# Two kinds of attention heads whose items alternate on one core

## What is computed

```
def diff_attention(q, k, v, lam):      # 6 heads, two components of width 32
    s = einsum('bqhcd,bkhcd->bhcqk', q, k) * DA ** -0.5
    p = softmax(s);  w = p[:, :, 0] - lam * p[:, :, 1]
    return einsum('bhqk,bkhe->bqhe', w, v)
def softmax_attention(q, k, v):        # 6 heads of width 96
    p = softmax(einsum('bqhd,bkhd->bhqk', q, k) * QK_C ** -0.5)
    return einsum('bhqk,bkhe->bqhe', p, v)
o_a = rmsnorm(diff_attention(...), subln_a) * (1 - l_init)
y = concatenate([o_a, conv, o_c]) @ w_out
```

## Time and profile before

| | us |
|---|---|
| median of 3 runs (lowest, highest) | 2022.19 (2021.28, 2024.68) |
| the profiled execution | 2023.35 |
| its span in the trace | 2021.3 |
| attention loop of layer 0, first score to first OC transpose | 217.7 to 402.3 |
| attention loop of layer 1 | 1119.9 to 1302.2 |

### The profile page before, as it was taken

The page is one execution under the profiler, slowest core; times in us unless marked ns, Lnnn a source line. Parts: engine busy times, 40 slices in busy tenths (PEclk is TensorE's granted clock), DMA queues, the critical chain, the costliest instruction groups (busy, mean ns, idle before and its releaser), DMA issues.

```text
span 2021.3 us, 28791 instructions
## 1 busy us (share of the span) xinstructions
PE 1836.7 (91%) x11300; PEld 1638.5 (81%) x11300; DVE 1407.1 (70%) x2038; ACT 1029.0 (51%) x1401; POOL 328.3 (16%) x507
## 2 busy tenths in 40 slices
PE   5999778799999999998998678897999999999994
PEld 3987666698999999998987566696788888888883
DVE  5375885537665656646466885536888888888987
ACT  4235686625121121124235786534777777777772
POOL 0082541001000000001083530200000000000002
PEclk9999799999999999999999899997999999999997
DMA  9125300023544445421221000006999999999995
GB/s 342 57 93 189 109 1 1 22 84 115 167 157 136 156 136 167 133 82 53 70 78 48 1 1 1 2 22 250 391 399 398 409 408 387 404 388 404 377 392 218
DMA packets 112438, 366.21 MB, mean 181 GB/s; under 512 B 7456, under 2 KB 65216, under 8 KB 85936
## 3 DMA queue, kind: packets, MB, share of 16 engines
q1 hardware_dynamic: 94448, 303.50, 40.1%
q0 software_dynamic: 13536, 48.39, 6.9%
q10 hardware_dynamic: 4320, 12.49, 1.6%
HBM read 349.23 MB, written 15.12 MB: 180 GB/s over the span
## 4 chain that ended last, share of the span: by engine, by line
PE 74%; DVE 13%; ACT 7%; DMA 3%; issue 2%; POOL 0%; SPq 0%; POOLq 0%; DVEq 0%; ACTq 0%
PE PS L2446 27%; PE PS L2335 25%; PE PS L2003 5%; PE PS L2390 5%; PE PS L2427 4%; ACT E L909 3%; PE PS L2126 3%; PE PS L2091 3%; DVE NM L1354 2%; DVE KCn L1301 1%; DVE split L1637 1%; ACT PT L914 1%; DMA raw<-in_w_ada_head 1%; DVE SS L1284 1%; DVE QC L1301 1%
## 5 line engine op out<-in xcount | busy, mean ns | idle before, releaser
L2446 PE MATMUL PS<-H,split 128*128 128x320 f32 x2304 | 339.7, 309 | 1.6 <-DVE H L1901 1.6
L2446 PEld LDWEIGHTS PS<-H,split 128*128 128x128 f32 x2304 | 338.1, 188 | 3.1 <-DVE H L1901 2.3
L1088 ACT CAST split<-raw 128x2048 fp32r<-128x2048 f32 (+2 forms) x64 | 112.8, 1763 | 228.5 <-PE PS L2446 184.4
L1637 DVE TENSOR_TENSOR split<-raw,split 128x2048 fp32r<-128x2048 f32 (+2 forms) x64 | 138.1, 2162 | 123.9 <-ACT split L1088 123.7
L1548 DVE TENSOR_TENSOR msplit<-raw,msplit 128x2048 fp32r<-128x2048 f32 x82 | 187.9, 2292 | 36.4 <-ACT msplit L1045 36.4
L1548 DVE TENSOR_TENSOR split<-raw,split 128x2048 fp32r<-128x2048 f32 x82 | 186.8, 2290 | 18.1 <-ACT split L1045 18.0
L2335 PE MATMUL PS<-split,HT 128*128 128x512 f32 x816 | 195.7, 396 | 3.7 <-DVE HT L1527 2.4
L1045 ACT CAST msplit<-raw 128x2048 fp32r<-128x2048 f32 x82 | 157.0, 1914 | 69.7 <-PE PS L2335 60.0
L2335 PE MATMUL PS<-msplit,HT 128*128 128x512 f32 x816 | 191.2, 390 | 0.6 <-DVE msplit L1548 0.6
L2003 PE MATMUL PS<-split,H 128*128 128x384 f32 (+1 forms) x960 | 171.3, 340 | 12.8 <-DVE split L1637 9.5
L2003 PEld LDWEIGHTS PS<-split,H 128*128 128x128 f32 x960 | 169.4, 195 | 14.5 <-DVE split L1637 10.7
(11 more groups left out here) (352 smaller groups left out, 3035.2 us busy)
## 6 DMA issues: line engine op xcount, KB each, us to landing
raw<-in_moe_w_gate SPq DMA_DIRECT2D x55, 1024.0 KB, 7.5
raw<-in_moe_w_down SPq DMA_DIRECT2D x55, 1024.0 KB, 7.9
raw<-in_moe_w_up SPq DMA_DIRECT2D x54, 1024.0 KB, 7.3
DOTW<-in_w_ada_rows POOLq DMA_DIRECT2D x56, 512.0 KB, 4.0
raw<-in_w_ada_head SPq DMA_DIRECT2D x16, 1024.0 KB, 7.0
mraw<-in_moe_w_up SPq DMA_DIRECT2D x14, 1024.0 KB, 7.3
mraw<-in_moe_w_gate SPq DMA_DIRECT2D x13, 1024.0 KB, 7.4
mraw<-in_moe_w_down SPq DMA_DIRECT2D x13, 1024.0 KB, 7.8
```

The costliest lines, as they stand in the source:

```text
L1088: A.copy(split[u % 2][:, 0, 0:w], src[:, 0:w]).then_inc(S["split_hi"], 1)
L1637: V.tensor_tensor(split[u % 2][:, 1, 0:w], src[:, 0:w], split[u % 2][:, 0, 0:w].bitcast(f32), ALU.subtract).then_inc(S["split_lo"], 1)
L2446: ins = T.matmul(PS[:, 4 * (u % 2) + 2 * c + hf, 0:HALF], W[:, w, k, c * P:(c + 1) * P], A(a, k, hf), start=(k == 0 and w == 0 and a == 0) ...
```

## The change

The items get a new order. Heads 0 and 1 run alone, then four blocks of ten alternate the items of heads 2 and 6, 3 and 7, 4 and 8, 5 and 9, then heads 10 and 11 run alone. Scores, semaphore values, outputs and groups now go by tables made from that order. Values of a block are paired within a kind (items 0 and 2, 1 and 3, 4 and 6, 5 and 7 of the block; 8 and 9 single), so that PT has a third buffer. LT leaves `split` and lies in two of the raw slots, those of the third and fourth w_out chunk, and SP loads these two only when the layer's last score is done. The subln work moves to the steps 50 to 55, two tiles a step; the mixing transposes to 55 to 59; the first chunk's rounding to 53 (ACT) and 54 (DVE).

```diff
-K_SUM, K_ROOT, K_NORM, K_OUT = A_ITEMS + 4, A_ITEMS + 14, A_ITEMS + 16, ITEMS - NT - 1
-K_MIX = ITEMS - NT - 2
+K_SUM, K_NORM = {50: (0,), 51: (1, 2), 52: (3, 4)}, {53: (0,), 54: (1, 2), 55: (3, 4)}
+K_ROOT, K_OUT, K_MIX, K_CONV = 52, 53, 55, 58
...
+BLOCKS = [(0, None), (1, None), (2, 6), (3, 7), (4, 8), (5, 9), (10, None), (11, None)]
+def item_list():
+    out = []
+    for a, c in BLOCKS:
+        for t in TILE_ORDER:
+            out += [(a, t)] if c is None else [(a, t), (c, t)]
+    return out
...
+            events = ((3, ("pair", 0, 2)), (4, ("turn", 0, 2)), (4, ("pair", 1, 3)), (5, ("turn", 1, 3)),
+                      (7, ("pair", 4, 6)), (8, ("turn", 4, 6)), (8, ("pair", 5, 7)), (9, ("turn", 5, 7)),
+                      (9, ("single", 8)), (10, ("single", 9)))
...
+    put(6, (7, 1), (8, 0), (8, 1))
+    for first, (a, c) in zip(range(10, 50, 10), BLOCKS[2:6]):
+        if a + 1 < HEADS:
+            put(a + 1, *((first + k, 0) for k in (-1, 0, 1, 3, 4, 5)))
+        put(c + 1, *((first + k, 0) for k in (2, 6, 7)))
...
-        PT = [at(f"PT{i}", [P, KEYS], OFF_H + 32256 + 2560 * i) for i in range(2)]
+        PT = [at(f"PT{i}", [P, KEYS], OFF_H + 32256 + 2560 * i) for i in range(3)]
...
-        LT = [at(f"LT{s}", [QK, (NT + KT_TILES) * P], OFF_SPLIT + s * 16384) for s in range(2)]
+        LTS = [[at(f"LT{l}_{s}", [QK, (NT + KT_TILES) * P], OFF_RAW + (LAYER_U[l] + U_OUT + 2 + s) % RAW_SLOTS * UNIT * 4)
+                for s in range(2)] for l in range(DEPTH)]
...
+                    if j == 2:
+                        sp.wait_ge(S["scored"], (l + 1) * SCORES)
                     load(base + U_OUT + j, w[:, :, j * 256:(j + 1) * 256], KC, 256)
...
+                if outputs_at(k):
+                    pe.wait_ge(S["ot_out"], l * pairs_before(ITEMS + 1) + pairs_before(k))
+                    if stored_before(k):
+                        pe.wait_ge(S["o_stored"], l * ITEMS + stored_before(k))
```

More of the change, by code:

```diff
@@ new lines, in comps_of, with outputs @@
+def comps_of(j):
+    return 2 if HEAD_AT[j] < HEADS else 1
+FIRST_SCORE = [sum(comps_of(i) for i in range(j)) for j in range(ITEMS)]
+A_INDEX = [sum(1 for i in range(j) if HEAD_AT[i] < HEADS) for j in range(ITEMS)]
+def score_of(j, c):
+    return FIRST_SCORE[j] + c
+def outputs():
+    at = {}
+    first = 0
+    for a, c in BLOCKS:
+        if c is None:
+            events = ((2, ("pair", 0, 1)), (3, ("turn", 0, 1)), (4, ("pair", 2, 3)), (5, ("turn", 2, 3)), (5, ("single", 4)))
+        else:
+            events = ((3, ("pair", 0, 2)), (4, ("turn", 0, 2)), (4, ("pair", 1, 3)), (5, ("turn", 1, 3)),
+                      (7, ("pair", 4, 6)), (8, ("turn", 4, 6)), (8, ("pair", 5, 7)), (9, ("turn", 5, 7)),
+                      (9, ("single", 8)), (10, ("single", 9)))
+        for k, (kind, *places) in events:
+            at.setdefault(first + k, []).append((kind, [first + j for j in places]))
+        first += NT if c is None else 2 * NT
+    return at
@@ L187, in outputs_at @@
+OUTPUTS = outputs()
 def outputs_at(k):
[L189 to L192, removed]
+    return OUTPUTS.get(k, [])
+STORE_ORDER = [j for k in sorted(OUTPUTS) for kind, places in OUTPUTS[k] if kind != "pair" for j in places]
+STORED = [STORE_ORDER.index(j) + 1 for j in range(ITEMS)]
 def outputs_ready(k):
-    return sum(1 for i in range(1, k + 1) if outputs_at(i))
@@ L200, in groups_of, with stored_before, pairs_before, turned_groups @@
-def groups_of(h):
-    return 6 if h < HEADS else 3
+    return sum(1 for i in OUTPUTS if i <= k)
+def stored_before(k):
+    return sum(len(places) for i in OUTPUTS if i < k for kind, places in OUTPUTS[i] if kind != "pair")
+def pairs_before(k):
+    return sum(1 for i in OUTPUTS if i < k for kind, _ in OUTPUTS[i] if kind == "pair")
+def turned_groups():
+    at = {}
+    def put(h, *steps):
+        for g, (k, place) in enumerate(steps):
+            at[k, place] = (h, g)
+    put(1, (-2, 0), (-1, 0), (0, 0), (0, 1), (1, 0), (2, 0))
+    put(2, (3, 0), (4, 0), (5, 0), (5, 1), (6, 0), (7, 0))
+    put(6, (7, 1), (8, 0), (8, 1))
[3 more added lines that the diff above has]
+        put(c + 1, *((first + k, 0) for k in (2, 6, 7)))
+    put(11, (49, 0), (50, 0), (51, 0))
+    return at
@@ L205, in groups_before, with group_place @@
+GROUPS_AT = turned_groups()
+GROUP_ORDER = [(0, g) for g in range(6)] + [GROUPS_AT[k] for k in sorted(GROUPS_AT)]
 def groups_before(h):
     return 6 * min(h, HEADS) + 3 * max(h - HEADS, 0)
+def group_place(h, g):
+    return GROUP_ORDER.index((h, g))
 def groups_at(k, place):
[L211 to L215, removed]
+    return GROUPS_AT.get((k, place))
@@ L843, in turn_out @@
             def turn_out(h, g):
[L845 removed]
+                act.wait_ge(S["turned"], l * TURNS + group_place(h, g) + 1)
                 s = h % 2
@@ L850, in turn_out @@
                 else:
-                    dst, first, end = LT[s], 512 * g, 11 * P
+                    dst, first, end = LTS[l][s], 512 * g, 11 * P
                 n = min(512, end - first)
@@ L1386, in mixer_dve @@
                             S["subln_sum"], 1)
-                if 0 <= k - K_NORM < NT:
-                    t = k - K_NORM
+                for t in K_NORM.get(k, ()):
                     if t == 0:
```

112 lines of the change are left out of this document (52 added, 60 removed).

## The result

| | before | changed |
|---|---|---|
| time, median | 2023.43 us (2021.28 to 2029.45, 4 runs) | 2057.24 us (2051.12 to 2060.14, 4 runs) |
| ratio to before | | 1.0159, 95% interval 1.014 to 1.0177 |
| profiled execution: span | 2021.3 us | 2058.1 us |
| mean granted clock of TensorE in it | 0.97 | 0.952 |

A forecast was written before the change was run, and what follows sets the result against it. The prediction took the loop of waits through a mixed block, not busy time, as the bound. Per layer 1.4 + 1.0 + 3.3 = +5.7, twice +11.4 on 2022.19, gave 2033 us, range 2012 to 2043.

The forecast's parts named there:

- The uncovered round trip to POOL: In mixed blocks DVE idles about 0.45 us ahead of the combination, waiting for POOL's factor, some 20 times per layer.
- The late loads: Loads of w_out chunks 3 and 4 at the layer's last score: free, with some 24 us of cover.
- The mixed block: Ten alternating differential and latent steps: the chain of waits takes 28.5 us a block, against 28.10 for two heads apart.
- the sum of 112.9: Four mixed blocks of a layer, 3 x 28.5 + 27.4 us, against 111.49 before: +1.4 per layer.
- The loop of waits: Chain across engines from latent score to latent score in a mixed block: 5.23 us for two items.
- bare walk: Stepping the read durations through a mixed block's waits, leaving out the 0.5 us for a combination stretched beside POOL.
- What costs nothing: Late loads, third PT buffer, LT's new place and wider waits ahead of values: no added time.
- the wider waits ahead of values: Waits ahead of value pairs: free, being on DVE work of earlier steps, done by then.
- The three groups of head 6: Turned groups now in steps 7 and 8 of a differential head: +1.0 us per layer, between 0 and 1.5.
- The end of the loop: Last steps, with root, scalings and rounding on DVE and ACT: 25.05 becomes 28.0 us, +3.3 per layer with two sums.
- PE fills up: Rival: PE's busy time bounds a mixed block at 24.1 us, 2000 in all; pays from below 26.8; chance 0.15.
- Port blocks in full: Rival: combinations wait out POOL's subtraction in mixed blocks, losing 1.1 us, not 0.5; +4 per layer, 2041; chance 0.15.

The follow-up runs named there:

- 6: The changed kernel with POOL's stack subtractions and additions held back until DVE's combination of that item is done: 2052.86 us, 1.0147.
- 5: The changed kernel with three of the nine turned groups of a mixed block done twice, ahead of PE's idle stretches: 2049.62 us, 1.0134.
- Experiment 1: The changed kernel with the old order of heads, groups, sums and norm; new LT place, third PT buffer and late loads stay: 2030.2 us, 1.0029.
- 7: The changed kernel with the norm's scaling one tile a step, steps 53 to 57, instead of one, two, two: 2053.77 us, 1.0145.
- 10: The changed kernel with the combination behind the next first maximum, norm one tile a step, and first latent head's groups one place earlier: 2026.4 us, 1.0009.
- 4: The changed kernel with every group of turns in steps 10 to 49 done twice on PE, same results: 2061.21 us, 1.0187.
- 2: The changed kernel with DVE's combination in mixed blocks moved behind the next step's first maximum: 2035.51 us, 1.0055.
- 3: The changed kernel with the combination's factor worked out on DVE by a tiny instruction instead of on POOL: 2042.91 us, 1.0104.
- 9: The changed kernel with the first latent head's groups of turns one place earlier: 2049.18 us, 1.012.
- 13: The kernel of 10 with three groups done twice in steps 29 to 49 and pair output turns three times from step 50: 2027.27 us, 1.0012.

## Why the prediction was right in direction and wrong in size

**What held.** The uncovered round trip to POOL was there 20 times a layer, 0.5 us each, as written. PE is idle about 5 us a block: 29.36 less 24.10 is 5.3 at full clock. DVE does not bound the block by busy time, and a block does not shrink to 24. The late loads cause no wait for raw in the loop.

**The step that failed** is "The mixed block", with its 28.5 us and the sum of 112.9. It took each duration of PE from rows at a granted clock of 1.00, and its text says nothing of the clock. The first two blocks took 30.5 and 30.4 us at a clock of 0.89, and the middle of the loop grew by 6.7 us in layer 1 where the sum had +1.4. At full clock they take 29.36 and 29.20. The loop of waits was near, in part by luck: 28.48 and 28.49 us in 6, with POOL's stacks held back, while the 28.5 holds 0.5 for a combination beside them. Put together for layer 1:

- clock: 1.16 us for each of three mixed blocks, 3.5. For the third block the 1.16 is from 5, where one group more is turned in it; no run had the changed kernel's own third block at 1.00.
- POOL beside the combination: 0.87 and 0.71 in the first two blocks (5 against 6), 1.6. The forecast had 0.5 a block of it, so it missed 0.6. The other 1.0 is its bare walk, some 0.5 a block too short.
- together 5.1 over the forecast's +1.4, against a measured 6.7 less 1.4, 5.3. That it closes so well is partly luck, since the third and fourth block are not split further.

A smaller term stood under "What costs nothing": the wider waits ahead of values. Experiment 1 has 1.0 us a layer at full clock there, 0.1 a value pair; how much of it is inside the walk's missing 0.5 is open.

**The other two terms.** "The three groups of head 6", +1.0, measured +3.3. Placing them one place earlier takes 1.8 off, and 1.5 is left, at the top of the forecast's range of 0 to 1.5. They ended one place too late, behind ACT's full list, and the first latent score waited for them. The wait is shown (1.29 us instead of 3.62); how much of the 1.8 it is worth is not. The clock has a part that I can't separate: with the same late groups the opening took 41.58 us at 0.83 here, 40.80 at 0.87 in 5 and 41.20 at 0.81 in 7, and in 10 the earlier groups gained 0 and 0.8. "The end of the loop", +3.3, measured +4.6. At full clock and with one tile a step it is 28.5, +2.2 over 26.34. The double scalings and the clock share the other 2.4 us. No run had the double scalings at full clock, so I do not split them.

In layer 1 the misses are 5.3, 2.3 and 1.3: 8.9 on a forecast of 5.7, which gives 14.6 of the 14.7 measured. Twice that is 29. The rest, 2 to 8 us outside the loops, was forecast as nothing and differs from one profile to the next (1654.3 and 1659.7 us for the same changed kernel, 1651.9 and 1652.6 for before). One part of it repeats: between the two loops the changed kernel took 720.29 and 720.18 us, the kernel before 716.35 and 716.15. Why is open, and so is what the edits left in 1 cost outside the loops.

**The rivals.** "PE fills up" was wrong for this order, and near in its condition: with the combination behind the next maximum, 26.5 us a block, the mixture wins back what opening and end lose, once these too are mended (10). It draws level with before; no order tried here beat it. "Port blocks in full" had the right place and a price that was too high: a combination grew by up to 0.72 us, not 1.1, for 0.6 a layer beyond what the forecast already held, not 4. The Trainium skill, "SBUF — State Buffer", section "Who interferes with whom", has a two-input DVE instruction contend with a GpSimd one that reads SBUF; the rows agree (1.60 us beside, 0.88 alone, 0.886 at most once the stacks wait).

**Why the clock falls** is shown in part. More work for PE in its idle stretches brought it back (5, and 4), and so did each edit that shortens the step (2, 3, 6), in all the first two blocks. That fits a clock that follows TensorE's activity. But the same code ran at 1.00 in one layer and at 0.89 in the other (7, 9), the third block of layer 0 fell in 2, 4, 5 and 6 too, and 13 did not hold the clock at layer 0's end. What comes before a block may have a part; which, stays open. The Trainium skill, "TensorE: Matmul & The Clock Gate", section "HAM oscillation — how this bites in real kernels", tells of a low clock that returns with each turn of a loop, where long waits for transfers stand between bursts of matmuls. Here it returns with each of three blocks, at a DMA share of 0.01 or less, and PE's longest idle row ahead of the half clock is 0.88 us in the first two blocks and 1.15 in the third.

## What to carry to other kernels

When two kinds of work are mixed to even out busy shares, look for the one small instruction that was covered by a neighbour (here 0.34 us on POOL), and put the next independent piece ahead of the wait for it. That edit alone gave back 22 of 34 us. Even so, the mixture here only drew level with the kernel before. When a change opens short gaps on TensorE, price its instructions at both levels of the granted clock, and check that column in every stretch before explaining a loss by waits.

## What was unexpected of the hardware

- A kernel that does the same transposes twice in three places of ten steps was not slower by the medians (2049.6 against 2057.2 us). Five of its six mixed blocks ran at a granted clock of 1.00, and its first two blocks were 1.2 us shorter than the changed kernel's at 0.89.
- The half clock can repeat with the program: in two executions of the changed kernel, 11 of 12 mixed blocks had one stretch at 1.2 GHz, and blocks at the same place were equal to 0.03 us. Small edits elsewhere put the first two blocks of one layer at full clock (7, 9).
